# The last eight products of a transformer trunk: two move from VectorE to GpSimd, six read a copied row

## The reference

```python
def rms_norm(x, g):
    xf = x.astype(jnp.float32)
    y = xf * lax.rsqrt(jnp.mean(xf * xf, axis=-1, keepdims=True) + RMS_EPS)
    return (y * g.astype(jnp.float32)).astype(x.dtype)
...
    for i in range(DEPTH):
        ...
        h = h + swiglu(rms_norm(h, ffn_norm[i]), ffn_w_gate[i], ffn_w_up[i], ffn_w_down[i])
    return rms_norm(h, final_norm)
```

## Time and profile before

| | us |
|---|---|
| median of three runs | 1129.24 |
| lowest and highest | 1128.73, 1129.81 |
| the profiled execution, its own time | 1129.83 |
| its span in the profile | 1128.0 |
| PE busy | 1107.0 (98%) |
| DVE busy | 581.5 (52%) |
| ACT busy | 331.0 (29%) |
| POOL busy | 51.1 (5%) |

### The profile page before, as it was taken

How to read it: one execution, slowest core, us unless ns; L and a number is a source line. 1 busy time by engine, 2 the same in 40 slices (tenths; PEclk the granted TensorE clock), 3 DMA queues, 4 the chain that set the end, 5 groups by cost and what they waited for, 6 DMA issues and landing times.

```text
span 1128.0 us, 13068 instructions
## 1 busy us (share of the span) xinstructions
PE 1107.0 (98%) x5040; PEld 920.2 (82%) x5040; DVE 581.5 (52%) x773; ACT 331.0 (29%) x398; POOL 51.1 (5%) x29
## 2 busy tenths in 40 slices
PE   8989999999999999999999999999999999999995
PEld 6878888888888888888888888888888888888884
DVE  6767774855445354333336456675444535433333
ACT  5557764332212122122222212232221222212220
POOL 4132221000000000000000000000000000000000
PEclk9989999999999999999999999999999999999998
DMA  5121120332222323322232332223223232222211
GB/s 204 58 76 46 57 75 38 112 112 92 94 98 88 112 74 112 103 94 80 98 112 75 112 112 75 102 85 112 103 83 106 81 110 77 109 103 103 77 54 74
DMA packets 17100, 103.98 MB, mean 92 GB/s; under 512 B 2032, under 2 KB 2032, under 8 KB 6576
## 3 DMA queue, kind: packets, MB, share of 16 engines
q1 hardware_dynamic: 16992, 103.33, 25.9%
q0 software_dynamic: 80, 0.26, 0.2%
HBM read 101.49 MB, written 2.10 MB: 92 GB/s over the span
## 4 chain that ended last, share of the span: by engine, by line
PE 96%; DVE 2%; DMA 1%; ACT 0%; issue 0%; SPq 0%; DVEq 0%; ACTq 0%
PE bank L360 31%; PE bank L362 31%; PE bank L361 31%; PE bank L489 1%; PE bank L503 1%; DMA xT<-xt 1%; DVE xT L1275 0%; PE bank L393 0%; PE bank L399 0%; PE bank L491 0%; DVE mid_lo L929 0%; DVE a_lo L969 0%; DVE w_lo L973 0%; DVE w_lo L886 0%; PE bank L407 0%
## 5 line engine op out<-in xcount | busy, mean ns | idle before, releaser
L360 PE MATMUL bank<-a_hi,w_hi 128*128 128x512 f32 x1000 | 392.8, 393 | 3.9 <-DVE a_lo L969 3.7
L361 PE MATMUL bank<-a_lo,w_hi 128*128 128x512 f32 x1000 | 389.9, 390 | 0.0
L362 PE MATMUL bank<-a_hi,w_lo 128*128 128x512 f32 x1000 | 389.8, 390 | 0.0
L646 ACT ACTIVATE w_hi<-raw 128x2048 fp32r<-128x2048 f32 (+2 forms) x99 | 181.3, 1831 | 651.1 <-PE bank L362 651.1
L886 DVE TENSOR_TENSOR w_lo<-raw,w_hi 128x2048 fp32r<-128x2048 f32 (+2 forms) x91 | 202.5, 2226 | 132.3 <-ACT w_hi L646 132.3
L360 PEld LDWEIGHTS bank<-a_hi,w_hi 128*128 128x128 f32 x1000 | 188.1, 188 | 45.4 <-DVE a_lo L969 3.3
L362 PEld LDWEIGHTS bank<-a_hi,w_lo 128*128 128x128 f32 x1000 | 188.1, 188 | 39.4
L361 PEld LDWEIGHTS bank<-a_lo,w_hi 128*128 128x128 f32 x1000 | 188.1, 188 | 39.4 <-issue 0.7
L360 PE MATMUL bank<-mid_hi,w_hi 128*128 128x512 f32 x496 | 194.1, 391 | 0.8 <-DVE w_lo L886 0.7
L362 PE MATMUL bank<-mid_hi,w_lo 128*128 128x512 f32 x496 | 193.1, 389 | 0.0
L361 PE MATMUL bank<-mid_lo,w_hi 128*128 128x512 f32 x496 | 193.0, 389 | 0.0
(11 more groups left out here) (123 smaller groups left out, 611.3 us busy)
## 6 DMA issues: line engine op xcount, KB each, us to landing
raw<-weights_in SPq DMA_DIRECT2D x82, 1024.0 KB, 4.8
raw<-weights_in SPq DMA_DIRECT2D x12, 768.0 KB, 4.2
raw<-weights_in SPq DMA_DIRECT2D x7, 512.0 KB, 3.8
xT<-xt SPq DMA_DIRECT2D x8, 256.0 KB, 7.6
out<-xT SPq DMA_DIRECT2D x8, 256.0 KB, 2.1
sin<-positions POOLq DMA_DIRECT2D x1, 256.0 KB, 6.5
vec<-vectors SPq DMA_DIRECT2D x1, 37.5 KB, 1.8
```

Source lines behind the costliest of these rows:

```text
L360: pe.matmul(o, lhs[0], rhs[0], start=start, stop=False, skip_group_check=True)
L361: pe.matmul(o, lhs[0], rhs[1], start=False, stop=False, skip_group_check=True)
L362: return pe.matmul(o, lhs[1], rhs[0], start=False, stop=stop, skip_group_check=True)
L646: act.activation(w_hi[s][:, 0:n], raw[s][:, 0:n], ACT.Copy).then_inc(hi_split[s], 1)
```

## The change

- After its last weight split, in the down projection's last round at c = 3, VectorE multiplies tiles 0 and 1 of `xT` by their gains, in place, and raises `weighted`.
- When bank 1 is complete, ScalarE copies it to `rstd` in SBUF and raises `rms_copied`.
- GpSimd waits for `rms_copied` and multiplies tiles 0 and 1 by `rstd`, and raises `pool_y_ready`.
- VectorE waits for `rms_copied` in place of `rms_spread`, and makes the products of tiles 2 to 7 only, with `rstd` in place of bank 1.
- SyncE issues the stores in the order 2, 3, 0, 4, 5, 1, 6, 7, each behind its semaphore.

```diff
-            for m in range(KD):
-                sp.wait_ge(y_ready, m + 1)
+            for ready, n, m in ((y_ready, 1, 2), (y_ready, 2, 3), (pool_y_ready, 1, 0), (y_ready, 3, 4), (y_ready, 4, 5),
+                                (pool_y_ready, 2, 1), (y_ready, 5, 6), (y_ready, 6, 7)):
+                sp.wait_ge(ready, n)
                 sp.dma_start(out[m * P:(m + 1) * P, :], tile(xT, m)).then_inc(out_stored, 16)
...
             split(1)
+            pool.wait_ge(rms_copied, 1)
+            for m in range(2):
+                pool.wait_ge(weighted, m + 1)
+                pool.tensor_tensor(tile(xT, m), tile(xT, m), rstd[:, :], ALU.mult).then_inc(pool_y_ready, 1)
...
             token_rms_of(0, D)
+            act.wait_ge(rms_spread, 2)
+            act.activation(rstd[:, :], bank[1][:, :], ACT.Copy).then_inc(rms_copied, 1)
...
                         if not (last and c >= 4):
                             split(c % 2, DOWN_AHEAD[c])
+                        if last and c == 3:
+                            for t in range(2):
+                                v.tensor_scalar(tile(xT, t), tile(xT, t), gain("final_norm", t), None, ALU.mult).then_inc(weighted, 1)
...
-            v.wait_ge(rms_spread, 2)
-            for m in range(KD):
-                v.scalar_tensor_tensor(tile(xT, m), tile(xT, m), gain("final_norm", m), bank[1][:, :], ALU.mult, ALU.mult).then_inc(y_ready, 1)
+            v.wait_ge(rms_copied, 1)
+            for m in range(2, KD):
+                v.scalar_tensor_tensor(tile(xT, m), tile(xT, m), gain("final_norm", m), rstd[:, :], ALU.mult, ALU.mult).then_inc(y_ready, 1)
```

More of the change, by code:

```diff
@@ L232, in build @@
         head_done = sem("head_done")
-        y_ready = sem("y_ready")
+        y_ready, pool_y_ready = sem("y_ready"), sem("pool_y_ready")
+        weighted, rms_copied = sem("weighted"), sem("rms_copied")
         out_stored = sem("out_stored")
```

## The result

The changed kernel takes 1132.38 us, the median of 8 runs (1131.89 to 1132.86), against 1129.57 us of the kernel before, 8 runs with it (1128.73 to 1130.4). The ratio is 1.0024, with a 95% interval of 1.0015 to 1.0033: 2.8 us slower. The forecast was 1131.2 us in a range of 1129.7 to 1132.4. The time lies just inside the upper edge of the range, and the case that came true is the rival "GpSimd first", which gave +2.7 us.

What follows compares the result with a forecast made beforehand. The prediction took the tail to be bounded by VectorE's products and the stores' drain, almost without slack. Copy 0.64 plus stores 1.33 gave +1.97 us, from 1129.24 to 1131.2 us, range 1129.7 to 1132.4.

Steps and rivals of the forecast that it cites:

- GpSimd first: Final products: GpSimd takes the inputs before VectorE, delaying tile 2's store; +2.7 us, median 1131.9, chance 0.17.
- What bounds the tail: After the last matmul: VectorE's products at 0.66 us pitch and stores draining at 0.684 us each, almost no slack between.
- The copy: Between last matmul and both engines: ScalarE's copy of the row to SBUF adds 0.64 us, bounds 0.5 and 0.7.
- The gain multiplications: Two VectorE multiplications after the split of c = 3, hidden in 11.62 us of idle time; cost 0.
- The stall: Final products, both inputs in SBUF: each GpSimd instruction holds VectorE up by 1.03 us, bounds 0 and 1.3.
- Who is first: Behind the copy: VectorE starts 0.04 us after ScalarE's record, GpSimd 0.08 us, so VectorE was taken as first.
- the stores' table: Eight stores in SyncE's order, with issue and movement times; the last ends at 8.43 against 7.10, +1.33 us.
- The main case: The tail with VectorE first and two stalls: copy 0.64 plus stores 1.33, +1.97 us, median 1131.2, chance 0.55.
- The side sums at other rates: Stores' term recomputed for faster drains: 1.1 us at 0.64 us per store, about 1.0 at 0.60.
- break-even: Stores' drain without a stall: it must fall by 0.08 us each for the change to break even.
- the faster case: No stall and stores following products in less than about 0.52 us each: -0.68 us, median 1128.6, chance 0.05.

Runs made afterwards that it cites:

- One product: Kernel before with seven of the eight final products left out, all eight stores issued behind the first product; +0.01 us from complete row to end, ratio 0.9997.
- two banks: Changed kernel with the row made twice, bank 1 for VectorE, bank 2 for the copy, stores ordered 2, 3, 4, 5, 0, 6, 1, 7; ratio to before 0.9995.
- store order: Changed kernel with the stores in the order 0, 2, 1, 3, 4, 5, 6, 7; +1.45 us against the kernel before, ratio 1.0012.
- bank input: Changed kernel with VectorE's six products reading bank 1 again, still behind the copy; +0.65 us against the kernel before, ratio 1.0006.
- head start: Changed kernel with a one-column memset on GpSimd between its wait for the copy and its first product; +1.95 us against the kernel before, ratio 1.0018.
- early half: Kernel before with the row made in halves, then whole, in three banks, tiles 0 to 2 multiplied and stored in halves; 1129.69 us against 1129.3, ratio 1.0003.

## Why the prediction came out as it did

- **What bounds the tail: right.** The forecast took the drain of the stores, 0.684 us each, as the floor, with VectorE just in front of it. One product shows it from one side (no products, no gain), two banks from the other (products 1.3 us sooner, no gain), and store order shows it inside the changed kernel.
- **The copy, 0.64 us: right.** It measured 0.63 alone and 0.65 with GpSimd's work beside it. No table load came with it.
- **The gain multiplications, 0: right.** In the changed kernel they stand in 0.88 us at 1098.25, and VectorE then waits another 10.83 us.
- **The stall, 1.03 us for each GpSimd instruction: right in kind, slightly small.** The two stalled records are 1.11 and 1.00 us above 0.74. The estimate came from GpSimd's additions, here it multiplies; the bank input run shows that it is the second SBUF input of VectorE that makes it.
- **Who is first: wrong.** The step "I take VectorE as first", drawn from starts 0.04 us (VectorE) and 0.08 us (GpSimd) after a ScalarE record, failed: GpSimd was first. The starts came as forecast (1120.65 and 1120.69), but with 0.04 us between them the order in which the records start does not decide; at 0.08 us, in the head start run, VectorE was first. The rows had a hint in the other direction, VectorE's split at 13.10 us beside GpSimd's addition at 13.07; I gave this case 0.17. This step alone is the difference between +1.97 and +2.7: the first store waits for a product that waits for GpSimd, and so the gap and the seven stores behind it all move: movement starts 1.03 us later, and the second gap of 0.3 us is gone.
- **The sizes in the stores' table: right.** For the case that came, the rival's last end was 9.14 us after the first product's start; measured about 9.25 (1129.9 - 1120.65). The main case measured +1.95 (head start) against +1.97.
- **The side sums at other rates: wrong, without effect.** Where the prediction lets the stores drain faster (0.64, 0.60, 0.52 us each, and the break-even 0.08 us lower), it still holds the kernel before at 7.10. At such a rate that kernel would end with its own last product instead, at 0.77 + 7 x 0.66 + 0.86 = 6.25 plus one store. With the same rate on both sides, the stores' term is 1.3 us at 0.64 and 1.2 at 0.60 (not 1.1 and 1.0), the break-even lies at 0.57 us each and the faster case at 0.47. The forecast uses none of them.
- **The point and the range.** Of the 1.2 us between 1131.2 and 1132.38, 0.7 are the failed step, and 0.33 are the reference itself, whose median is 1129.57 over eight runs and not the 1129.24 of the first three. The chances said 0.34 for a loss above 0.2%; 0.24% came, in an interval from 0.15% to 0.33%. That the time lies within the range is luck in part: the range's high end was set by the rival's case plus 0.5 us, the measured time is 0.02 us below it, and the case given 0.55 is not the one that came. The interval reaches 0.09% to each side, so less than the 0.2% that the prediction named can be told from none (store order: 0.12%, 0.03% to 0.21%).

The Trainium skill's rule in "SBUF — State Buffer", section "Who interferes with whom", names the kind of pair that stalls, two SBUF inputs on VectorE beside a GpSimd instruction that reads SBUF, and the bank input run agrees with it from the other side: with one SBUF input there is no stall, and GpSimd's instruction is as it was. The section also says that whoever issues first blocks the other. Taken by the start of the records, that agrees with the head start run, and not with the three profiles in which VectorE's record led by 0.04 or 0.05 us and was the blocked one. The blocked product waited 1.11 us beside a GpSimd record of 1.26 us, somewhat less than the whole of it.

What stays open: why GpSimd is served first although its record starts 0.04 us later. A lead of 0.04 to 0.05 us was too little in three profiles, and one of 0.08 us enough in one, where a memset stood before GpSimd's product and its record ended 0.12 us after VectorE's start, so the real lead may have been larger. Whether it is the time from a record's start to its first read, or a preference of the chip, none of these runs tells apart.

## What to carry to other kernels

Before splitting the last products between engines, look at what comes after them: if the share of the transfers is at 1 from the first store on, faster products gain nothing (bank input, one product, two banks), and anything that delays the first store or opens a gap behind it is paid in full. Moving an operand of VectorE from a bank to SBUF is not neutral beside a GpSimd that reads SBUF: two GpSimd instructions took 2.1 us from VectorE here, more than the two products that they replaced (1.3 us). Where two engines are released by the same semaphore and share something, work out both orders, and choose the order of what follows, here the stores, so that it fits the worse one: that alone was worth 1.3 us.

## What the runs showed of the hardware that was not expected

- A lead of 0.04 to 0.05 us of VectorE's record over GpSimd's left GpSimd first (three profiles); 0.08 us, with the memset in between, put VectorE first (one profile). The difference for the kernel was 0.8 us.
- SyncE's issue of a 256 KB store takes 0.33 to 0.35 us where stores follow each other at 0.66 us (before, store order), and in one product, where they are issued back to back, first 0.35 to 0.45 and then 0.64 to 0.66 us, which is nearly the 0.684 us in which one drains.
- Issued back to back by SyncE, stores of 128 KB (early half) follow each other at 0.4 to 0.5 us, and so do the first five of 256 KB (one product), so halves did not keep the transfers full. A half moved at about 353 GB/s and a whole store at 383 GB/s while one of them filled the transfer engines.
